# Feed-forward token halves as contiguous columns, whole matmuls in unit 0, and another order of the norm's steps

## The reference, cut to what matters

```
x = x + 0.5 * swiglu(rms_norm(x, ffn1_norm), w_gu, w_down)     # first
x = x + mixer(x)                                               # delta rule and attention
x = x + 0.5 * swiglu(rms_norm(x, ffn2_norm), w_gu, w_down)     # second

def rms_norm(x, g): return x * rsqrt(mean(x * x, -1) + EPS) * g
def swiglu(x, w_gu, w_down):
    gate, up = split(x @ w_gu, 2, axis=-1)
    return (silu(gate) * up) @ w_down
```

## Time and profile before

| | us |
|---|---|
| median of 3 runs | 1507.66 (1506.07 to 1507.8) |
| the profiled execution | 1512.05 |
| its span | 1510.3 |
| PE busy in it | 1413.5 (94%) |
| DVE, ACT, POOL busy | 939.3, 624.8, 333.2 |
| mean granted clock of PE | 0.967 |

### The profile page before, as it was taken

How to read it: one execution, slowest core, us unless ns; L and a number is a source line. 1 busy time by engine, 2 the same in 40 slices (tenths; PEclk the granted TensorE clock), 3 DMA queues, 4 the chain that set the end, 5 groups by cost and what they waited for, 6 DMA issues and landing times.

```text
span 1510.3 us, 24805 instructions
## 1 busy us (share of the span) xinstructions
PE 1413.5 (94%) x8869; PEld 1268.5 (84%) x8869; DVE 939.3 (62%) x1549; ACT 624.8 (41%) x1161; POOL 333.2 (22%) x246
## 2 busy tenths in 40 slices
PE   6999999999997999999988878689899999999999
PEld 5999999988786998787776765467899999998787
DVE  5777777744446776547646765633677777764444
ACT  5444444433335543433253432433354444443333
POOL 2544444300000000212122221001244444410000
PEclk8999999999998999999998999899899999999999
DMA  5222233180101422101040025660023232316000
GB/s 183 57 84 83 83 84 90 48 310 7 28 0 37 145 57 88 56 29 57 1 148 7 1 78 198 236 214 28 29 84 84 83 83 84 87 62 241 12 23 35
DMA packets 139127, 126.25 MB, mean 84 GB/s; under 512 B 3909, under 2 KB 107973, under 8 KB 139068
## 3 DMA queue, kind: packets, MB, share of 16 engines
q1 hardware_dynamic: 136556, 116.11, 24.3%
q0 software_dynamic: 2512, 9.34, 1.8%
HBM read 114.79 MB, written 10.39 MB: 83 GB/s over the span
## 4 chain that ended last, share of the span: by engine, by line
PE 85%; DVE 10%; ACT 3%; issue 2%; DMA 1%; POOL 0%; SPq 0%; DVEq 0%; ACTq 0%
PE psum_all L873 25%; PE psum_all L875 24%; PE psum_all L874 24%; PE psum_all L1801 2%; PE psum_all L1814 1%; PE psum_all L1917 1%; ACT pr L2131 1%; PE psum_all L1806 1%; DMA K_c<-cache_k 1%; PE psum_all L2177 0%; PE psum_all L2167 0%; DVE hB_lo L549 0%; DVE x_tok L868 0%; DVE pc L2107 0%; PE psum_all L2050 0%
## 5 line engine op out<-in xcount | busy, mean ns | idle before, releaser
L873 PE MATMUL psum_all<-hB_hi,gq_hi 128*128 128x320 f32 (+2 forms) x1312 | 403.7, 308 | 1.2 <-DVE hB_lo L549 1.2
L874 PE MATMUL psum_all<-hB_lo,gq_hi 128*128 128x320 f32 (+2 forms) x1312 | 403.0, 307 | 0.0
L875 PE MATMUL psum_all<-hB_hi,gq_lo 128*128 128x320 f32 (+2 forms) x1312 | 401.6, 306 | 0.0
L496 DVE TENSOR_TENSOR gq_lo<-raw_gu,gq_hi 128x512 fp32r<-128x512 f32 x240 | 192.6, 804 | 99.7 <-ACT gq_hi L492 99.0
L873 PEld LDWEIGHTS psum_all<-hB_hi,gq_hi 128*128 128x128 f32 x1312 | 249.3, 190 | 2.0 <-DVE hB_lo L549 2.0
L874 PEld LDWEIGHTS psum_all<-hB_lo,gq_hi 128*128 128x128 f32 x1312 | 249.4, 190 | 0.0
L875 PEld LDWEIGHTS psum_all<-hB_hi,gq_lo 128*128 128x128 f32 x1312 | 249.3, 190 | 0.0
L492 ACT ACTIVATE gq_hi<-raw_gu 128x512 fp32r<-128x512 f32 x240 | 150.7, 629 | 151.5 <-POOL raw_gu L464 95.3
L689 DVE TENSOR_TENSOR a_lo<-aT,a_hi 128x640 fp32r<-128x640 f32 x88 | 72.6, 825 | 169.3 <-ACT a_hi L681 169.3
L873 PE MATMUL psum_all<-wd_hi,a_hi 128*128 128x512 f32 x440 | 172.6, 392 | 1.6 <-DVE x_tok L868 1.6
L875 PE MATMUL psum_all<-wd_hi,a_lo 128*128 128x512 f32 x440 | 173.5, 394 | 0.0
(11 more groups left out here) (346 smaller groups left out, 2474.9 us busy)
## 6 DMA issues: line engine op xcount, KB each, us to landing
raw_gu<-ffn_w_gu SPq DMA_DIRECT2D x88, 512.0 KB, 4.6
wd<-ffn_w_down SPq DMA_DIRECT2D x2, 4096.0 KB, 21.8
raw_b<-w_in SPq DMA_DIRECT2D x8, 1024.0 KB, 5.2
K_c<-cache_k SPq DMA_DIRECT2D x8, 1024.0 KB, 8.5
V_c<-cache_v SPq DMA_DIRECT2D x8, 1024.0 KB, 5.5
raw_cv<-w_in SPq DMA_DIRECT2D x13, 512.0 KB, 4.0
wd<-ffn_w_down SPq DMA_DIRECT2D x2, 3072.0 KB, 14.1
wd<-ffn_w_down SPq DMA_DIRECT2D x4, 1024.0 KB, 15.6
```

The lines of the kernel that those rows point to most:

```text
L496: nc.vector.tensor_tensor(gq_lo[i][:], operand(slot, i), raw(gq_hi[i][:]), ALU.subtract)\
L873: nc.tensor.matmul(out, lhs_hi, rhs_hi, start=start, stop=False, skip_group_check=True)
L874: nc.tensor.matmul(out, lhs_hi, rhs_lo, start=False, stop=False, skip_group_check=True)
L875: return nc.tensor.matmul(out, lhs_lo, rhs_hi, start=False, stop=stop, skip_group_check=True)
```

## The change

Half 0 is now tokens 0 to 319 and half 1 tokens 320 to 639. Block (model-width half, token half) is then a plain slice of an array in token order: `hT_hi` and `hB_lo`, `[8, 640]`, with the combined blocks in `tB_hi` and `tB_lo`. `halves` and `by_tile` go; DVE and ACT write and read 128 or 320 columns in a row where it was 64.

```
+        def h_block(x, i):
+            return x[:, 4 * (i // 2):4 * (i // 2) + 4, HALF * (i % 2):HALF * (i % 2) + HALF]
         def h_rows(x, t, half):
-            return x[:, 2 * half:2 * half + 2, :, 64 * t:64 * t + 64]
+            return x[:, 4 * half:4 * half + 4, t * P:(t + 1) * P]
...
-                nc.vector.tensor_tensor(odd, by_tile(u3[:]), by_tile(p5[:]), ALU.add)\
+                nc.vector.tensor_tensor(odd, u3[:], p5[:], ALU.add)\
```

```
-            for part in range(2):
-                pe.wait_ge(*s.n.lo((6, 2 * TT)[part]))
+            for a in range(2):
+                pe.wait_ge(*s.n.lo((6, 2 * TT)[a]))
                 for q in range(4):
                     pe.wait_ge(*s.sums(q + 1))
-                    last = plain(0, q, PARTS[part])
-                    if part == 1:
+                    last = plain(0, q, a)
+                    if a == 1:
                         last.then_inc(s.mm.sem, 1)
-                    elif q == 1:
+                    elif q == 0:
                         ffn_norm_pe(pe, s, (4,))
```

```
             inverse(2)
+            scale(2)
             residual(3)
+            gain(1)
             h_lo(dve, s, 0)
-            scale(2)
-            gain(1)
+            gain(2)
             residual(4)
             h_lo(dve, s, 1)
             inverse(3)
             scale(3)
-            gain(2)
             h_lo(dve, s, 2)
             inverse(4)
             scale(4)
             gain(3)
+            gain(4)
             h_lo(dve, s, 3)
-            gain(4)
             h_lo(dve, s, 4)
```

```
+            if not early:
+                act.wait_ge(*n.var(0))
+                nc.scalar.activation(silu_gate[:, 0:1], stats[:, 1, 0:1], ACT.Sqrt)
...
+            sp.dma_start(x_tok[:, 0, :], x_in[:, 0, :]).then_inc(s_x[0], 16)
             sp.dma_start(ident, io["consts"][:, 0:P]).then_inc(s_ident, 16)
-            sp.dma_start(x_tok[:, 0, :], x_in[:, 0, :]).then_inc(s_x[0], 16)
+            sp.dma_start(x_tok[:, 1, :], x_in[:, 1, :]).then_inc(s_x[1], 16)
             sp.dma_start(gains[:], io["gains"]).then_inc(s_gain, 16)
```

More of the change, by code:

```diff
@@ L405, in operand, with h_hi_of, h_lo_of @@
                     r[:, 1, 4:8])[i]
[L407 to L415, removed]
+        def h_block(x, i):
+            return x[:, 4 * (i // 2):4 * (i // 2) + 4, HALF * (i % 2):HALF * (i % 2) + HALF]
+        def h_hi_of(i):
+            return h_block(hT_hi, i) if i < 4 else tB_hi[:, i - 4]
+        def h_lo_of(i):
+            return h_block(hB_lo, i) if i < 4 else tB_lo[:, i - 4]
         def ffn_raw(sp, s, w_gu, j, slot):
@@ L542, in h_hi @@
                 act.wait_ge(*s.cp(2 * t + half + 1))
-                nc.scalar.activation(h_rows(hB_hi, t, half), h_rows(h32, t, half), ACT.Copy)\
+                nc.scalar.activation(h_rows(hT_hi, t, half), h_rows(h32, t, half), ACT.Copy)\
                     .then_inc(s.n.hi.sem, 1)
@@ L609, in gain @@
                     h_gain(dve, s, t, half)
+            if not early:
+                nc.vector.memset(stats[:, 1, :], 1.0).then_inc(n.var.sem, 1)
             residual(0)
@@ L778, in even_odd @@
             def even_odd(j):
-                return (halves(aT[:, j, :])[:, h] for h in range(2))
+                return (aT[:, j, h * HALF:(h + 1) * HALF] for h in range(2))
             def unit(j, slot, last=False):
@@ L812, in unit @@
                 dve.wait_ge(*s.product(j, 6))
[L813 removed]
+                nc.vector.tensor_tensor(even, u3[:], psum[b + 3][:, 0:HALF],
                                         ALU.subtract).then_inc(s.vec.sem, 1)
@@ L878, in ffn_pe, with product @@
         def ffn_pe(pe, s):
[L879 removed]
+            def product(slot, i):
                 for k in range(KT // 2):
[L881 to L883 removed]
+                    last = three(psum[4 * slot + SLOT_OF[i]][:, 0:HALF], gq_hi[i][:, k, :],
+                                 gq_lo[i][:, k, :], h_hi_of(H_OF[i])[:, k, :],
+                                 h_lo_of(H_OF[i])[:, k, :], OPENS[i] and k == 0,
                                  k == KT // 2 - 1)
```

68 lines of the change are left out of this document (32 added, 36 removed).

## The result

The changed kernel takes **1484.92 us** (median of 4 runs, 1483.3 to 1488.62) beside 1506.87 for the kernel before (4 runs, 1504.4 to 1507.8): ratio 0.986, interval 0.9837 to 0.9884. A second comparison gave 1488.09 (4 runs) beside 1505.52 (15 runs), ratio 0.9888, interval 0.9844 to 0.9931. So the gain is about 17 to 22 us.

A forecast was written before the change was run, and what follows sets the result against it. PE was taken as the bound, with 85% of the span; 7.6 us less in the first feed-forward and 6.8 in the second made 14.4, taking the median of 1507.66 to 1493.3 us, range 1488.5 to 1499.

The forecast's parts named there:

- Part 1, whole matmuls: Unit 0: 96 matmuls of 320 columns replace 96 of 192 and 96 of 128; 7.5 us less per feed-forward.
- Part 2, the clock: Unit 0 lasts its full-clock 14.8 us plus half the half-clock time: 17.6 us in both feed-forwards.
- c: Time in us at half clock after unit 0's first product; taken as 5.7 in both feed-forwards.
- its lower bound: Shortest half-clock time after unit 0's first product, about 3 us, as products may start right behind tile 3's transposes.
- Part 3, the first product: Head of each feed-forward: first product 0.2 us later in the first, at 22.6, and 0.4 later in the second.
- The upper bound: Latest first product in the first feed-forward, 23.3, with the load no earlier and low parts taking a full 4.0.
- Part 4, operands in time: Unit 0's second half, units 1 and 2: PE does not wait for tile 4 or weights; costed at nothing.
- The sum: First feed-forward 7.6 us less, second 6.8; all engines then hang on PE, so 14.4 us stays.
- the first one: Rival: tile 0's low parts slip past POOL and half clock lasts 3 us in both; 1488.5, chance 0.17.
- Supply: Rival: tile 4's low parts and weights of units 1 and 2 come no earlier; 1498.0 to 1499.3, chance 0.16.
- columns don't set the spacing: Denies the rival that unit 0's matmul cost goes by columns, so whole matmuls gain nothing; 1508.3, chance 0.03.
- the clock did not stay down: Denies the rival that PE waits and the clock stays at 1.2 GHz through unit 0; 1517.3, chance 0.03.

The follow-up runs named there:

- a_split: Changed kernel with each unit 0 product issued as 192 and 128 columns again, part of the sums left out; 1502.71 us, ratio to before 0.998.
- b_again: Kernel before, profiled again without any edit; no run time given, its middle (first feed-forward's unit 1 to the mixer's output projection) took 1003.8 us.
- b_again2: Kernel before, unedited, profiled once more; no run time given, its middle took 999.9 us.
- b_again3: Kernel before, unedited, profiled once more after that; no run time given, its middle took 995.6 us.
- a_again: Changed kernel, profiled again without any edit; no run time given, its middle took 999.0 us.
- a_poolquiet: Changed kernel with POOL's first two low parts of unit 0's weights replaced by writing zeros; 1485.47 us, a single run.
- a_oldnorm: Changed kernel with the norm's DVE order, first root and load order as before; 1491.5 us, ratio 0.9907 to the kernel before.
- a_oldorder: Changed kernel with only DVE's norm order as before, new loads and first root kept; 1487.58 us, ratio 0.9888.
- a_ord2: Changed kernel with DVE making tile 3's variance and scale ahead of tile 1's low parts; 1490.13 us, ratio 0.989.
- b_newnorm: Kernel before with only the changed norm: DVE's order, dummy root, load order; 1501.1 us beside 1504.27, ratio 0.997.
- a_fill: Changed kernel with 48 extra identity transposes on PE behind the transposes of tiles 0, 1 and 2; 1485.9 us, ratio 0.9868.
- a_late: Changed kernel with 60 extra identity transposes and ACT's second high part of the weights made later; 1487.19 us, ratio 0.9883.

## Why the prediction had the sign but not the size

- **Part 1, whole matmuls: right.** 7.5 us per feed-forward: 96 products where 192 stood, 0.147 apart at full clock where it was 0.111 to 0.113, no idle in front of any, and a_split gives the gain back.
- **Part 2, the clock: the step that failed most.** I gave both feed-forwards a c of 5.7, the mean of the two that one execution of the kernel before showed, so 2.85 us over the 14.8 of full clock; the profile after has 16.74 and 15.55, so 1.9 and 0.75. That is 0.9 + 2.1 = 3.0 us of the 4.2 that the heads gave beyond the 14.4. Two things were wrong. A 320-column matmul at the lower clock stands 0.267 apart, not twice 0.146, so a us there loses 0.45 us, not 0.5. And c is shorter. By the clock records of the traces it is, in us from the first product to the rise:

  | profiles | first feed-forward | second |
  |---|---|---|
  | before, b_again, b_again2, b_again3 | 6.4, 6.9, 5.5, 4.5 | 5.0, 4.6, 4.4, 4.7 |
  | after, a_again, a_poolquiet (320 columns, no wait) | 3.7, 4.2, 1.4 | 1.1, 1.4, 1.7 |
  | a_oldnorm, a_oldorder, a_ord2 (320 columns, PE waits) | 3.6, 3.9, 6.2 | 4.8, 4.8, 4.9 |
  | b_newnorm, a_split (192 and 128 columns, no wait) | 3.8, 7.5 | 4.4, 7.7 |

  "Wait" is PE's idle time for low parts between tile 3's transposes and the first product. The 6.4 that I took from the first feed-forward lies near the top of what that kernel shows itself. In the second the prediction had a sign of the shorter c in hand, as its lower bound (about 3): products start right behind tile 3's transposes. With 320-column products unit 0 takes 17.24, 17.24 and 17.31 there in the three kernels with the wait (0.6 to 1.0 us), and 15.05 to 15.82 in the five profiles without it (the two lowest, a_fill and a_late, with PE's gap filled as well). The 1.1 measured lies below even that bound. In the first feed-forward a wait of 0.6 us makes no difference: unit 0 takes 16.66 and 16.85 with it (a_oldnorm, a_oldorder), 16.74 and 16.99 without it.
- **Part 3, the first product: the first feed-forward wrong by 1.2 us, the second right.** DVE's chain went as worked out, step by step (gain 9.09, scale of tile 2 10.90, low parts 12.77 and 3.23 long, scale of tile 3 18.93); it began 0.73 earlier, because tile 1's square was taken at 7.35 and began at 6.62. I let the load take as long as before. From tile 0's low parts to tile 3's scale it then took 6.16 where 6.5 was worked out, which is most of the rest. a_oldorder shows that the head start, and not DVE's order, moves the first product. It is not steady, though: tile 1's variance came between 7.49 and 8.76 in the nine profiles with the new loads, and between 8.89 and 9.41 in the five with the old ones. The upper bound is 22.6 + 0.35 + 0.5 = 23.45 by its own terms, not 23.3; nothing hung on it. In the second feed-forward 0.3 later was measured and 0.4 predicted.
- **Part 4, operands in time: right.** No idle in front of tile 4's transposes or the second half's products.
- **The sum** "from there on all engines hang on PE, so it stays" is right for the rest of the first feed-forward (413.7 to 413.8 before, 413.9 after) and roughly on the mean for the mixer, but not for one execution: the middle of the kernel before spreads over 11 us by itself. My range allowed for unknown costs of the change alone. The three runs that I had (1506.07 to 1507.8) showed little of a spread that 36 later runs put at 1499.9 to 1510.4; the profiled execution, 4.4 us over their median, was a hint that I passed over. The time is 8.4 us under the forecast: 0.8 because the kernel before came out at 1506.87 instead of 1507.66, 3.7 in the heads (18.1 by their means, 14.4 forecast), and 3.9 that the heads do not hold and that lie within the mixer's spread. With the heads alone the time would have been 1489.6, inside the range.
- **The rivals.** No rival came to pass whole. Of the first one the early clock did (c of 3.7 and 1.1 where it had 3 in both), but the collision with POOL that it denied is real. Supply held; columns don't set the spacing (a_split); the clock did not stay down.

**Still open.** What sets the length of the slow stretch. In the second feed-forward it is short only where 320-column products and no wait come together; either alone leaves c at 4.4 to 7.7. In the first feed-forward a wait of 0.6 us plays no part, and why c is 3.6 to 4.2 there, where the kernel before has 4.5 to 6.9, is not shown. DVE's order (a_oldorder against the changed kernel) takes the wait away together with a start 0.3 us later; no edit took it away alone. And why the mixer's share at the lower clock differs by as much as it does between executions of one kernel was not tried.

## What to carry to other kernels

Where narrow matmuls stand at a fixed distance, choose the split of the columns so that all of them are wide: one spacing row foretold 14.8 us for unit 0 at full clock, and a_fill has 15.05. A wait of half a us in front of the products went with 1.6 us more of unit 0 in the second feed-forward here, for a start only 0.3 us later without it; it cost nothing of the kind in the first, so try it rather than count on it. And before a range is given, look at how far the kernel before spreads from one execution to the next, stage by stage.

## What the hardware showed that I had not expected

- **The granted-clock column says 1.00 where the trace holds no clock record.** Windows of PE in the profile after:

```profile
14.00:21.30 7.30, 1.56 (x8) 1.00 0.35 104
21.36:25.20 3.84, 3.84 (x17) 1.00 0.15 38
```

  The column says 1.00, but the first clock record of this trace begins at 25.10. The products ahead of it stand 0.267 us apart, those behind it 0.147. That 0.267 is the lower clock is shown by a_oldnorm, whose records reach further back. Its window of PE, in which 320-column products stand 0.267 apart as well:

```profile
22.95:26.05 3.10, 3.10 (x11) 0.50 0.00 0
```

  So the mean clock of a page can leave out a slow stretch at the start, and the spacing of equal matmuls is the surer row.
- **A DVE operation that reads two SBUF tiles waits out a POOL operation that reads SBUF, but not one that only writes it**: 3.23 beside two subtractions of POOL, 2.19 beside one (a_late), and 1.29 beside its zeros. The Trainium skill, page "SBUF — State Buffer", section "Who interferes with whom", states just this, and the trace agrees. A scale, which reads one SBUF tile, takes longer as well: 0.75 alone, 1.84 beside POOL in a_late; that POOL is the cause there is read from the overlap in time alone.
- **One kernel's middle varied by 11 us of about 1000** from one execution to another, with the same matmuls; 9 of the 11 us are PE's own busy time (936.05 against 927.03).
